# Two models' blocks on one core: where the norm scales' product is issued, and how gate/up hands over to its output product

## The reference, cut to what matters

```python
def rms_norm_2(x, g, eps=EPS):
    xf = x.astype(F32_2)
    y = xf * lax.rsqrt(jnp.mean(xf * xf, axis=-1, keepdims=True) + eps)
    return (y * g.astype(F32_2)).astype(x.dtype)

def swiglu(x, w_gate, w_up, w_down):
    return (jax.nn.silu(x @ w_gate) * (x @ w_up)) @ w_down

        h = swiglu(rms_norm_2(x, ng[0]), ffn_w_gate[l, 0], ffn_w_up[l, 0], ffn_w_down[l, 0])
        x = x + 0.5 * rms_norm_2(h, ng[1])
```

## Time and profile before

| | us |
|---|---|
| median of 3 runs | 3486.66 |
| lowest, highest | 3476.53, 3487.84 |
| the profiled execution's own time | 3479.5 |
| its span, first to last instruction | 3477.7 |
| PE busy | 2912.1 (84%) |
| DVE busy | 2455.1 (71%) |
| ACT busy | 775.0 (22%) |
| mean granted TensorE clock | 0.927 |

### The profile page before, as it was taken

How to read it: one execution, slowest core, us unless ns; L and a number is a source line. 1 busy time by engine, 2 the same in 40 slices (tenths; PEclk the granted TensorE clock), 3 DMA queues, 4 the chain that set the end, 5 groups by cost and what they waited for, 6 DMA issues and landing times. The chain is left out here.

```text
span 3477.7 us, 45455 instructions
## 1 busy us (share of the span) xinstructions
PE 2912.1 (84%) x17776; PEld 2292.3 (66%) x17776; DVE 2455.1 (71%) x4591; ACT 775.0 (22%) x1982; POOL 626.6 (18%) x520
## 2 busy tenths in 40 slices
PE   8789978777777889677777769998887999998898
PEld 8678963333333689333333329997777999997898
DVE  7262677777777886877777878775436887867686
ACT  4114122222222342122222221013222101023300
POOL 0000014444445100344444540000000000000000
PEclk9899988889888999888899889999999999999999
DMA  6253559999999734899999996543203565652364
GB/s 205 87 183 102 192 208 421 411 411 415 401 403 421 260 117 166 352 415 410 408 419 391 406 394 179 188 146 122 85 5 124 168 194 167 192 171 91 115 194 152
DMA packets 469127, 859.91 MB, mean 247 GB/s; under 512 B 18736, under 2 KB 398512, under 8 KB 402224
## 3 DMA queue, kind: packets, MB, share of 16 engines
q0 software_dynamic: 73728, 536.90, 37.5%
q1 hardware_dynamic: 394896, 319.85, 29.1%
q10 hardware_dynamic: 288, 0.24, 0.0%
HBM read 848.55 MB, written 8.39 MB: 246 GB/s over the span
## 5 line engine op out<-in xcount | busy, mean ns | idle before, releaser
L2477 PE MATMUL banks<-arena,arena 128*128 128x512 f32 x1744 | 913.5, 682 | 356.4 <-ACT arena L2546 356.4
L2477 PEld LDWEIGHTS banks<-arena,arena 128*128 128x128 f32 x1744 | 371.1, 220 | 880.0 <-ACT arena L2546 441.1
L2435 POOL DMA_INDIRECT arena<-in_peer_uv,arena x512 | 621.6, 1214 | 1380.6 <-DVE arena L2663 684.9
L2701 DVE CUSTOM_DVE_ANT_0 arena<-arena,normed 128x1024 f32<-128x1024 f32 x512 | 625.7, 1222 | 234.4 <-DMA arena<-in_peer_uv,arena 232.0
L410 DVE TENSOR_TENSOR weight_ring_part<-weight_ring,weight_high_parts 128x2048 fp32r<-128x2048 f32 (+2 forms) x244 | 539.9, 2213 | 8.4
L3246 PE MATMUL banks<-normed_columns_part,weight_high_parts 128*128 128x256 f32 x1408 | 392.8, 279 | 1.5 <-DVE weight_ring_part L410 1.1
L3247 PE MATMUL banks<-normed_part,weight_high_parts 128*128 128x256 f32 x1408 | 390.9, 278 | 0.0
L3248 PE MATMUL banks<-normed_columns_part,weight_ring_part 128*128 128x256 f32 x1408 | 390.9, 278 | 0.0
L772 PE MATMUL banks<-weight_high_parts,arena_part 128*128 128x256 f32 x1216 | 341.7, 281 | 36.4 <-PEq L350 23.5
L407 DVE CAST weight_high_parts<-weight_ring 128x2048 fp32r<-128x2048 f32 (+2 forms) x244 | 289.8, 1188 | 104.9 <-PE banks L774 82.3
L773 PE MATMUL banks<-weight_ring_part,arena_part 128*128 128x256 f32 x1216 | 339.3, 279 | 0.0
(11 more groups left out here) (574 smaller groups left out, 4354.9 us busy)
## 6 DMA issues: line engine op xcount, KB each, us to landing
weight_ring<-in_ffn_w_gate SPq DMA_DIRECT2D x88, 512.0 KB, 3.7
weight_ring<-in_ffn_w_up SPq DMA_DIRECT2D x88, 512.0 KB, 4.9
weight_ring<-in_ev_w_in SPq DMA_DIRECT2D x33, 1024.0 KB, 5.4
weight_ring<-in_ffn_w_down SPq DMA_DIRECT2D x32, 1024.0 KB, 5.0
weight_ring<-in_od_w_in SPq DMA_DIRECT2D x23, 1024.0 KB, 5.3
weight_ring<-in_xa_wkv SPq DMA_DIRECT2D x16, 1024.0 KB, 5.6
weight_ring<-in_peer_wq SPq DMA_DIRECT2D x16, 1024.0 KB, 5.2
weight_ring<-in_ev_w_out SPq DMA_DIRECT2D x12, 1024.0 KB, 5.4
```

The lines of the kernel that those rows point to most:

```text
L2435: pool.indirect_dma_start(out=ring[:, slot(i, s), :], out_offset=None, in_=table, in_offset=bass.IndirectOffsetOnAxis(ap=index[:, i % 2, s ...
L2477: mm = pe.matmul(k.ps[:, 2 * b + half, :], diag[:, g % 2, s, :], v, start=n == b * PEER_TOPK, stop=n == last_mixed[b])
L2701: dve.tensor_tensor_reduce(out=ring[:, here, 0:D], in0=ring[:, here, 0:D], in1=k.xn[:, i % NB, :], scale=1.0, scalar=0.0, op0=ALU.mult, op ...
```

## The change

`scale_tensor` is moved: in `ffn` behind block 3 instead of block 1; in `columns_out` without `tensor_then` behind block 3 (or the last, if there are fewer); in `rows_out` without `tensor_then` behind the second tile. Products with `tensor_then` stay as they are.

`ffn` keeps its step open (`hold=True`), so no engine meets another between gate/up and `land`. In its place `land` gets `follows`: SP waits for the squares' signal of before (the gain row's memory was used for them), PE waits at the start until 21 of the 22 hidden chunks have been taken from their banks, and before each use of hidden chunks for the first time until their two parts are there: once for all 8 chunks of the first weight tile, once for those of the second, and chunk by chunk for the last six.

```diff
@@ def land(..., also=None, follows=False):
             @block.sync
             def _(sp):
                 if post is not None:
+                    if follows:
+                        sp.wait_ge(self.squared.sem, self.squared.start)
                     self.load_row(sp, post)
...
             def _(pe):
+                columns_at = self.columns_split.start - 2 * kc
+                if follows:
+                    pe.wait_ge(self.evacuated.sem, self.evacuated.start - 1)
...
                             for c in range(n):
                                 k = t * KC + c
+                                if follows and j == 0 and b == 0 and (t == per - 1 or c == 0):
+                                    pe.wait_ge(self.columns_split.sem, columns_at + 2 * (k + 1 if t == per - 1 else (t + 1) * KC))
@@ def columns_out
-                    if fresh and m == 1:
+                    if fresh and m == (min(3, len(parts) - 1) if tensor_then is None else 1):
                         self.scale_tensor(pe)
@@ def rows_out
-                    if fresh and j == 0:
+                    if fresh and j == (min(1, len(widths) - 1) if tensor_then is None else 0):
                         self.scale_tensor(pe)
@@ def ffn(k, l, i, nxt):
-    with k.step() as block:
+    with k.step(hold=True) as block:
...
-                if m == 1:
+                if m == 3:
                     k.scale_tensor(pe)
...
-    k.land(hidden_parts, FF_CHUNKS, nxt, post=f"norm_g_{l}{post}", factor=0.5, unscaled=True)
+    k.land(hidden_parts, FF_CHUNKS, nxt, post=f"norm_g_{l}{post}", factor=0.5, unscaled=True, follows=True)
```

More of the change, by code:

```diff
@@ L706, in scaled, with land @@
         self.pending, self.unsquared, self.first_norm = False, False, False
-    def land(self, xT, kc, nxt=None, dst=None, post=None, factor=1.0, unscaled=False, also=None):
+    def land(self, xT, kc, nxt=None, dst=None, post=None, factor=1.0, unscaled=False, also=None, follows=False):
         per = -(-kc // KC)
```

## The result

The changed kernel takes 3518.37 us (median of 4 runs, 3517.32 to 3521.78) beside 3482.64 us for the kernel before in the same comparison: ratio 1.0105, 95% interval [1.0084, 1.0126], 36 us slower. The forecast was 3521, +38. The profiled execution took 3517.32 us, its span 3515.4 (before 3477.7), the mean granted clock is 0.920 (before 0.927). Lines behind 731 have moved: L772 is now L783, L945 is L956, L2136 is L2147, L3246 to L3248 are L3257 to L3259, L3285 is L3296, L3297 is L3308.

The account below looks back on a forecast made before the run. PE, busy 84% of the span, bounds the kernel where it stands still. Moved product +28.9, removed meeting -9.7 and clock +18.8 give +38 us: 3521, the middle between profiled and median bases; range 3500 to 3538.

Parts of the forecast that it names:

- The chain behind the product: From L696 through ACT's and DVE's queues to tile 2's first matmul: PE idles; the move costs +28.9 us at full clock.
- the mixer's +4.5: Odd mixer's query product: the move costs +4.5 us, as DVE has 0.5 us of small work before its first reading.
- What of the old wait stays: Ahead of tile 1, whose split PE still needs: 2.5 of the 3.5 us wait at the scales' product remain.
- `rows_out` was +0.6: In `rows_out`, product behind the last tile and ACT's four readings behind `wide`: 9.5 us becomes 10.2, +0.6.
- The meeting: Between gate/up and `land`: four gaps of 2.95, 1.84, 2.95, 2.41 us shrink to 0.11 each, -9.7 us.
- The possible wait at tile 1 of `land`: DVE's split of that tile may come late, up to 0.6 us a place, 2.4 in all; kept for the range only.
- The clock: All nine long idle stretches drop PE's clock over what follows: 7 x 2.2 + 2 x 1.7 = +18.8 us, bounds 0 and +32.
- the upper bound: Clock term at +32 us: 2.64 at every drop, and 1.7 behind the five waits of 2.5 us.
- Whether tile 2's parts are there in time: Rival at block 4's first matmul: split done when PE comes, old waits vanish, -44.7 us, 3435; chance 4%.
- That the clock holds: Rival: no clock drops behind the idle stretches, +19.2 us, 3499 on the profiled base, 3506 on the median; chance 17%.
- That every wait drops it: Rival: every wait lowers the clock and tile 1 of `land` is late too, +54 us, about 3537; chance 10%.
- The wash: Rival: the chain behind L696 shrinks and the clock gains, so the move costs less than 20 us in all; chance 4%.

Follow-up runs that it names:

- The early split: Changed kernel, with DVE splitting weight tile 2 before it waits for the spread scales: 3480.64 us, ratio 0.9997 against the kernel before.
- both halves: Against the kernel before: only the meeting removed, 3469.58 us, ratio 0.9957; only the scales' product moved, meeting kept, 3527.93 us, ratio 1.0135.
- the best version: The early split with the product behind block 2 (in `rows_out` behind the first tile, as before): 3459.48 us, ratio 0.9941 against the kernel before.
- the extra rounded matmul: The best version plus one ordinary 128x256 matmul with rounded operands at the start of `land`: 3460.3 us, ratio 0.9952 against the kernel before.

## Why the prediction was right

**The chain behind the product.** From L696 to the first matmul of tile 2 the prediction read 6.89 us; it is 6.78 in all four feed-forwards. In the query products of 8 blocks it read 5.43, measured 5.32; in the odd mixer 5.90 and 5.79. The 0.11 less in each lies between L696 and ACT's copy (0.62 instead of 0.73): the product's two records start 0.22 us apart now, in the flow of matmuls, and 0.32 us apart behind a stop. One sum was off by little: the trace before has 1.70 us in the second query product and 1.74 in the odd mixer between tiles 0 and 1, so that the mixer's +4.5 should have been +4.3.

**What of the old wait stays** was read as 2.50 us in five places: 2.50, 2.51 and 2.32 in the feed-forwards, 2.51 and 2.50 in the queries of four blocks. From the end of tile 0 to the first score these were forecast at 12.56 us and took 12.55. `rows_out` was +0.6; between the same two points it is +0.4 (9.55 to 9.96 us), and +0.2 from its first matmul on.

**The meeting** was -9.7. The four gaps sum to 0.46 instead of 10.15: -9.7. The possible wait at tile 1 of `land` did not come, since PE was behind DVE by more in all four places, as the prediction had it.

**The clock** was the term with the widest bounds, and it came out place by place. All nine long stops were followed by the lower clock. Tile 2 behind them took 8.13, 7.59, 7.19 and 7.28 us in the feed-forwards, 8.4 too much in all against 8.8 forecast. In the queries of the first model and the odd mixer it cost 1.7, 1.7 and 2.6 us, 6.0 against 6.6. Behind the wait for the scores, the scores themselves ran 1.85 and 1.97 us longer, 3.8 against 3.4. Together 18.3 of 18.8. In two places tile 1 ran slow behind the wait of 2.5 us (7.06 and 7.17 us from first to last matmul instead of 5.33), 3.6 us that stood only in the upper bound; behind the other three waits of that length the clock held. The rule of the Trainium skill that was weighed (TensorE: Matmul & The Clock Gate, "What's actually happening") and the trace agree on the long stops: nine of nine were followed by the lower clock.

**The sum.** Feed-forwards: +28.6 from the first matmul of gate/up to the last, of 24.5 forecast; the difference is the slow tile 1 and 1.5 us more of slow clock in the very first tile, less small change. The other six places: +16.3 within their stages and +3.8 in the scores, 20.1 of 23.2; the 3 us less are mostly pace, since the first queries and the odd mixer ran at 117.8 before and run at 113.3 behind the stop now. The meeting: -9.7. Not forecast: the pace of the output products, +6.7. That makes +45.7 where the span grew by 37.7; the missing -8.0 lies in stretches that the change does not touch (-2.8 between the second queries and the first feed-forward, -2.5 between the first output product and the third queries, the rest in smaller pieces), and was not followed further. So the mechanism and its terms came out, but that the total did so to within a microsecond is luck: +4.1, -3.1, +6.7 and -8.0 cancelled.

**The rivals.** Whether tile 2's parts are there in time was named as the point that decides. The early split made just that case, and the whole loss went. That the clock holds is refuted by the stretches above. That every wait drops it, those of 2.5 us too, is refuted by three of the five of that length, and tile 1 of `land` was not late. The wash is refuted by both halves measured apart (+47, -11).

## What to carry to other kernels

When a wait is moved later, follow the queue of the engine that needs its result, and look for what has nothing to do with it but stands behind it in order: here two instructions of weight splitting behind an evacuation. Most of the wait that the profile put down to the product belonged to another step (the split of tile 1), so moving the product could not remove it. Reordering the consumer's queue, tile 2's split ahead of the wait for the scales, is what made a later product pay.

## What the runs showed of the hardware that was not expected

Uninterrupted matmuls of 256 columns at a granted clock of 1.00 have two paces here, 113.3 and 117.8 ns from start to start, and keep one for hundreds of matmuls. For the 1056 matmuls of a gate/up that is 4.7 us, for the 528 of an output product 2.3. What was seen to change it:

- *A stop.* The pace can change or not: in the two kernels that move the product and keep the meeting, 117.8 was followed by 113.4 three times and by 117.8 once, 113.3 by 113.4 three times and by 117.8 once. A wait of 0.4 us is enough. At tile 1 of `land` the pace went from 117.8 to 113.3 in three of five such waits (two in the best version, one with the extra rounded matmul) and stayed in two.
- *The junction from gate/up to the output product, without a stop.* It changed over at each of 24, four of them with an extra rounded matmul between.
- *A plain float32 matmul in the flow.* Behind it the pace was 117.8, whatever it was ahead: 47 of 47 at L696, 4 of 4 at the junction.

Why is open, and the last two were not separated from all else: the operands change sides at the junction (the weights are the loaded operand before it and the streamed one behind it), which was not tried by itself.

The Trainium skill (TensorE: Matmul & The Clock Gate, "Wait — 56ns, not 53.3ns?") gives one figure for back-to-back matmuls, the columns at 2.4 GHz and about 2.5 ns, by which 256 columns would take an estimated 109 ns. Both measured paces lie above it, and there are two; for these operands the measurement decides.
